# Multiplications of constants in front of TensorE's waits in a three-layer mixed kernel

## The chip, the cores and the metric

The kernel runs on one core of one Trainium2 chip. The metric is the device time of one execution in microseconds (us), from the start of the program to its end.
## What is computed

256 tokens of width 1024 go through two layers of a first block and one layer of a second. Cut to what matters:

```python
# first block: conditioning by adaLN, two layers
mod = silu(c) @ ada_w[layer] + ada_b[layer]        # six rows of 1024: shifts, scales, gates
h = modulate(rmsnorm(x, g), sh1, sc1)
# layer 0: Mamba-2 scan (both directions) beside 2-D neighbourhood attention, 16 heads
# layer 1: mLSTM, 8 heads, both directions
x = x + g1 * rmsnorm(mixer(h))                     # then the same around the MLP of width 4096
# second block, one layer
proj = rmsnorm(x) @ w_in                           # Fox attention, S5, HGRN2 and three gates
merged = g0 * (y_fox @ wb0) + g1 * (y_s5 @ wb1) + g2 * (y_hg @ wb2)
x = x + merged @ w_out
x = x + cross_attention(rmsnorm(x), rmsnorm(mem))  # 4 heads of width 256
x = x + swiglu(rmsnorm(x), w_gate_up, w_down)
```

All is float32. The large products are made from two halves of each operand (high and low), in three passes.

## The kernel before, in words

All weights come as one stream of chunks (4 tiles of 128 rows by 512 columns, 1 MB), loaded by SP into a ring of seven. For each chunk ScalarE writes the high half (`split_hi`, L1193), VectorE the low half (`split_lo`, L1204), and TensorE multiplies: L1020 where the tokens are stationary ("tok"), L1028 where the weights are ("feat"). `Product` is one weight matrix; `PRODUCTS` gives their order: mem, in0, out0, up0, down0, in1, out1, up1, down1, in2, glu, fox_out, s5_out, hg_out, mix_out, xq, xo, gate_up, swi_down. Results go to PSUM banks in pairs, and ScalarE and VectorE take them.

Smaller work (scans, softmax heads, norms) is woven between the chunks: each engine runs a generator per stage, and `Woven` advances those of the guests by a table of due steps (`paced`). So the order on every engine is fixed when the program is built, and an engine that waits holds up all that stands behind it. At the end of each stage of `all_stages` the engines meet (`meet`, L4226: drain, then wait for all three).

The names that the change touches:

- `guest_columns` (L979 to L990): the adaLN rows. VectorE sums a weight chunk over its rows (L1115, L1118) in eight steps; TensorE then adds over the partitions with a matrix of ones (L987, two columns each). There are 24 such guests, n = 0 to 23, spread over mem, in0, up0, down0, in1, out1 and up1.
- `PostProduct` and `Join`: the end of a mixer or an MLP and the norm that starts the next part. After a meeting VectorE makes the rate (L495 to L509), adds to x (L1453), ScalarE squares (L1430), TensorE transposes x in four banks (L1410), VectorE makes the second rate, TensorE lays it out as a row (L1416), and VectorE and ScalarE make the operand (L1471, L1441, L1464), tile by tile. `GainRow` (L1313) lays out the gate's row. There are four joins: before up0, in1, up1 and in2.
- `TurnHalves` and `LateNorm`: transposes of the merged branches and of x (L810) for mix_out, xq and gate_up.
- `Ssd`: the products of C and B (L1845) and the transposes of the convolved x (L1859). ScalarE makes `silu_in` (L1924) and `x_taken` (L1934).
- `Neighbours`: per head scores (L2159), softmax on VectorE and ScalarE, transposes of the shares (L2169), values (L2185). `Mlstm.turn` (L2438), `Hgrn` (L3094), `QkNorm` for Fox (L3259, after GpSimd's L3243) and `CrossAttention` (sums L3785, scores L3794, transposes L3805) are of the same kind.

The order of waits in four of these places, by the program: in `Ssd` half 1, `silu_in` at 3, then `x_taken`; in `TurnHalves`, `ready(j)` (the product's group), then `freed` (`key_in` at 4, from L3707 and L3709); in the sums of `CrossAttention`, ScalarE's and VectorE's take of the queries, then `probs_taken`; in the Fox transposes, `qk_scaled`, then `copied`.

Of the kernel before, what the change touches and what calls it, by code (L numbers as in the profile page):

```python
# [65 lines left out]
def ada_groups(layer, part0, part1):  # L66
# [32 lines left out]
          "out1": [3], "up1": [3, 9]}  # L99
FIRST_PARTS = [(0, 0), (1, 0), (0, 1), (1, 1)]  # L100
# [437 lines left out]

class MemLead(Stage):
# [257 lines left out]
class TurnHalves(TurnIn):  # L797

    def __init__(self, k, src, scale, ready, freed=()):  # L800
        super().__init__(k, src, KD, k.h_hi, k.h_lo, scale, ready)
        self.freed = freed
# [49 lines left out]
class LateNorm(TurnHalves):  # L852

    def __init__(self, k, gain, halves, junk, small, rate_row=None):
# [3 lines left out]
        super().__init__(k, k.x, lambda f: gain[:, f:f + 1], lambda j: halves(j // 2))  # L859
# [60 lines left out]
class Product(Stage):  # L920
# [9 lines left out]
    def __init__(self, k, name, src, act_out, dve_out, act_after=None, dve_after=None, is_split=False,  # L930
                 guest=None, lead=()):
        super().__init__(k)
        self.name, self.lead = name, lead
# [58 lines left out]
    def tensor(self, pe):  # L992
# [46 lines left out]
        if self.own:  # L1039
            self.guest_columns(pe, len(self.own) - 1)  # L1040

# [296 lines left out]
class PostProduct(Product):  # L1338

    def __init__(self, k, name, src, y, junk, small, guest=None):
        super().__init__(k, name, src, True, True, guest=guest)
        self.y, self.junk, self.small = y, junk, small
# [41 lines left out]
class Join(Stage):  # L1385
# [14 lines left out]
    def tensor(self, pe):  # L1400
        k, m = self.k, self.m
        if self.gain is not None:
            self.gain.lay_out(pe)
        for j in range(4):
# [7 lines left out]
        for wait in self.post.taken():  # L1412
            pe.wait_ge(*wait)
        pe.wait_ge(*m["rate_in"].at(2))
# [3 lines left out]
        mm.then_inc(m["rate_laid_out"].sem, 1)  # L1418

# [392 lines left out]
class Ssd(Stage):  # L1812
# [18 lines left out]
    def tensor(self, pe):  # L1831
# [8 lines left out]
        for _ in range(6):  # L1840
            yield
        pe.wait_ge(*m["silu_in"].at(1))
# [8 lines left out]
        for half in range(2):  # L1851
            pe.wait_ge(*m["silu_in"].at(half + 2))
            for t in range(TT):
                if half == 0:
                    pe.wait_ge(*m["cb_taken"].at(t + 1))
                else:
                    pe.wait_ge(*m["x_taken"].at(t + 1))
# [273 lines left out]
class Neighbours(Stage):  # L2131
# [20 lines left out]
    def tensor(self, pe):  # L2152
# [199 lines left out]
class Mlstm(Stage):  # L2352
# [31 lines left out]
    def tensor(self, pe):  # L2384
# [45 lines left out]
        def turn(h, products):  # L2430
            pe.wait_ge(*m["head_gated"].at(4 * (h // 2) + 4))
            pe.wait_ge(*m["ml_copied"].at(products))
            if h >= 1:
                pe.wait_ge(*m["mixed_lo"].at(2 * h))
            for f in range(2):
# [119 lines left out]
def layer1_stages(k, mods, base, small, guest, post, more):  # L2555
# [62 lines left out]
    def act_after(act, st, i):  # L2618
        kind, n = order[i]
        if kind == "o":  # L2620
# [10 lines left out]
                  lead=(join, Columns(k)))  # L2631
    gate.follow(in1)
    cell = Mlstm(k, qT, kT, v, o, sel, gate, h, e, sc, sm, junk, hi, lo, first, k.guests, o_in)
    out1 = PostProduct(k, "out1", cell, y, junk2, small, guest)
# [417 lines left out]
class Hgrn(Stage):  # L3052
# [30 lines left out]
    def tensor(self, pe):  # L3083
# [4 lines left out]
        for i, c, half in self.steps():  # L3088
            if i >= 2:
                pe.wait_ge(*m["took"].at(i - 1))  # L3090
            pe.wait_ge(*m["ops"].at(i + 1))
# [125 lines left out]
class QkNorm(Stage):  # L3217
# [514 lines left out]
class CrossAttention(Stage):  # L3732
# [38 lines left out]
    def tensor(self, pe):  # L3771
        k, m = self.k, self.m

        def sums(g):
# [4 lines left out]
            else:  # L3779
                pe.wait_ge(*m["probs_taken"].at(2))  # L3780
# [143 lines left out]
def block2_stages(k, base, small, keep, s5, post):  # L3924
# [93 lines left out]
    def glu_act_after(act, st, i):  # L4018
# [14 lines left out]
                        [key_norm.m["key_in"].at(4)])  # L4033
# [3 lines left out]
    norm_x = LateNorm(k, k.par("norm_x"), halves(mix_out), rows(at_gl + TT * D), small[:, 80:96])  # L4037
# [38 lines left out]
def all_stages(k, bias, kept):  # L4076
# [78 lines left out]
    out0 = PostProduct(k, "out0", src, y, junk, small)  # L4155
# [33 lines left out]
def mlp(k, layer, mod, base, small, guest, post, more=()):  # L4189
# [17 lines left out]
    down = PostProduct(k, f"down{layer}", Operand(None, uo.hi, uo.lo, hidden.made), y, junk, small, guest)  # L4207
# [98 lines left out]
```

## Time and profile before

| | us |
|---|---|
| median of three runs | 1708.2 (1707.31 to 1708.4) |
| the profiled execution | 1710.6 |
| its span, first to last instruction | 1708.8 |
| TensorE busy | 1574.6 (92%) |
| VectorE busy | 1162.8 (68%) |
| ScalarE busy | 791.3 (46%) |
| GpSimd busy | 59.2 (3%) |

The busy share in 40 slices of 42.7 us each, in tenths, with the granted clock of TensorE and the share of the DMA engines:

```profile
PE   6978997998999979999899997999989989899998
...
DVE  6788866447776596676777566899873585556653
...
PEclk9978998998999989999999998999998999999999
DMA  9775552323766645434546553322332343244552
```

A row of the chain of work names an engine, a tile and a line with its share of the span. A row of the waits reads: who waited, for what, how long in total, how often, the longest. A row of a table by stretches gives the stretch in us from the span's start, its length, the busy time and number of instructions of each engine, the granted clock, the share of the DMA engines and what they moved. A row of the timeline gives start, duration, engine, line, operation, output and inputs, with the idle time before it and its cause in brackets.

### The profile page before, as it was taken

How to read it: one execution, taken by the hardware profiler on the slowest of the kernel's cores; microseconds unless marked ns; L12 is line 12 of the kernel's file. 1: busy time of each engine (PE TensorE's matmuls, PEld its weight loads, DVE VectorE, ACT ScalarE, POOL GpSimd, SP SyncE). 2: the span in 40 equal slices, each digit the busy share in tenths (PEclk: the TensorE clock that was granted, in tenths of full speed). 3: DMA queues.
4: the chain of work that ended last, by engine and by line, in shares of the span. 5: the costliest groups of instructions: out<-in, count | busy, mean ns of one | idle time of the engine just before them, and what ended most of it. 6: DMA issues, size and time to landing. Idle time of an engine off the chain costs nothing.

```text
span 1708.8 us, 22579 instructions
## 1 busy us (share of the span) xinstructions
PE 1574.6 (92%) x9002; PEld 1330.9 (78%) x9002; DVE 1162.8 (68%) x1837; ACT 791.3 (46%) x1069; POOL 59.2 (3%) x72
## 2 busy tenths in 40 slices
PE   6978997998999979999899997999989989899998
PEld 5768885568998778987699886866765678789997
DVE  6788866447776596676777566899873585556653
ACT  4453464445453344545355533655533544344442
POOL 0000000000000000000000003440010000000000
PEclk9978998998999989999999998999998999999999
DMA  9775552323766645434546553322332343244552
GB/s 389 304 272 201 222 199 94 114 99 105 277 234 246 268 176 221 148 124 138 206 167 229 177 193 123 125 98 99 123 124 74 148 148 136 86 145 177 182 187 74
DMA packets 41367, 292.83 MB, mean 171 GB/s; under 512 B 4528, under 2 KB 4784, under 8 KB 6704
## 3 DMA queue, kind: packets, MB, share of 16 engines
q1 hardware_dynamic: 40112, 284.04, 45.1%
q10 hardware_dynamic: 1152, 7.34, 1.1%
q8 instruction: 73, 1.20, 0.3%
q14 instruction: 30, 0.25, 0.0%
HBM read 288.22 MB, written 3.15 MB: 171 GB/s over the span
## 4 chain that ended last, share of the span: by engine, by line
PE 72%; DVE 17%; ACT 5%; issue 3%; DMA 2%; POOL 1%; DVEq 0%; SPq 0%; ACTq 0%; POOLq 0%
PE ps L1020 31%; PE ps L1028 26%; DVE ring_at_lo L1204 5%; ACT w_hi L1193 2%; DVE arena_at L1118 2%; PE ps L2886 1%; DMA ring_at<-stream 1%; PE ps L2427 1%; DVE arena_at L2008 1%; PE ps L3094 1%; PE ps L1883 1%; PE ps L2185 1%; PE ps L987 1%; PE ps L2873 1%; PE ps L2159 1%
## 5 line engine op out<-in xcount | busy, mean ns | idle before, releaser
L1204 DVE TENSOR_TENSOR ring_at_lo<-ring_at,w_hi 128x2048 fp32r<-128x2048 f32 (+1 forms) x218 | 495.8, 2275 | 212.9 <-ACT w_hi L1193 212.8
L1193 ACT ACTIVATE w_hi<-ring_at 128x2048 fp32r<-128x2048 f32 (+1 forms) x218 | 414.5, 1902 | 244.0 <-PE ps L1020 158.1
L1028 PE MATMUL ps<-h_hi,w_hi 128*128 128x256 f32 x1440 | 419.2, 291 | 8.7 <-DVE hT_at_lo L1464 6.4
L1028 PE MATMUL ps<-h_hi,ring_at_lo 128*128 128x256 f32 x1440 | 419.6, 291 | 0.0
L1028 PE MATMUL ps<-hT_at_lo,w_hi 128*128 128x256 f32 x1440 | 414.8, 288 | 0.0
L1020 PE MATMUL ps<-w_hi,arena_at_lo 128*128 128x512 f32 x1232 | 395.9, 403 | 3.7 <-ACTq L4226 2.5
L1028 PEld LDWEIGHTS ps<-h_hi,w_hi 128*128 128x128 f32 x1440 | 283.0, 197 | 18.9 <-issue 18.5
L1020 PEld LDWEIGHTS ps<-w_hi,arena_at_lo 128*128 128x128 f32 x1232 | 233.7, 193 | 61.5 <-issue 6.2
L1028 PEld LDWEIGHTS ps<-h_hi,ring_at_lo 128*128 128x128 f32 x1440 | 281.2, 195 | 0.0
L1028 PEld LDWEIGHTS ps<-hT_at_lo,w_hi 128*128 128x128 f32 x1440 | 279.0, 194 | 0.3
L1020 PE MATMUL ps<-ring_at_lo,arena_at_lo 128*128 128x512 f32 x616 | 246.5, 400 | 0.0
L1020 PE MATMUL ps<-w_hi,h_hi 128*128 128x512 f32 x368 | 155.9, 424 | 0.0
L1020 PE MATMUL ps<-ring_at_lo,h_hi 128*128 128x512 f32 x368 | 146.2, 397 | 0.0
L1020 PE MATMUL ps<-w_hi,hT_at_lo 128*128 128x512 f32 x368 | 146.1, 397 | 0.0
L1020 PEld LDWEIGHTS ps<-ring_at_lo,arena_at_lo 128*128 128x128 f32 x616 | 117.7, 191 | 27.2
L1118 DVE SCALAR_TENSOR_TENSOR arena_at<-ring_at,cond,arena_at 128x512 f32<-128x512 f32 x168 | 125.9, 749 | 3.9
L1020 PEld LDWEIGHTS ps<-w_hi,h_hi 128*128 128x128 f32 x368 | 70.5, 192 | 24.0 <-issue 10.6
L1020 PEld LDWEIGHTS ps<-ring_at_lo,h_hi 128*128 128x128 f32 x368 | 70.1, 190 | 17.5
L1020 PEld LDWEIGHTS ps<-w_hi,hT_at_lo 128*128 128x128 f32 x368 | 70.4, 191 | 13.2
L2934 POOL TENSOR_SCALAR arena_at<-con,arena_at 128x256 f32<-128x256 f32 x16 | 12.1, 753 | 1087.6 <-DVEq L4226 1049.3
L987 PE MATMUL ps<-ones,arena_at 128*128 128x2 f32 x192 | 25.2, 253 | 22.9 <-DVE arena_at L1118 22.9
L987 PEld LDWEIGHTS ps<-ones,arena_at 128*128 128x128 f32 x192 | 25.4, 203 | 26.0 <-DVE arena_at L1118 25.5
(458 smaller groups left out, 1664.0 us busy)
## 6 DMA issues: line engine op xcount, KB each, us to landing
ring_at<-stream SPq DMA_DIRECT2D x266, 1024.0 KB, 4.8
arena_at<-bias ACTq DMA_DIRECT2D x4, 768.0 KB, 6.1
kept<-arena_at ACTq DMA_DIRECT2D x2, 1024.0 KB, 11.9
arena_at<-kept ACTq DMA_DIRECT2D x2, 1024.0 KB, 7.5
arena_at<-mem SPq DMA_DIRECT2D x1, 1024.0 KB, 7.5
x_res<-x SPq DMA_DIRECT2D x1, 1024.0 KB, 17.4
out<-x_res SPq DMA_DIRECT2D x2, 512.0 KB, 2.8
con<-consts SPq DMA_DIRECT2D x1, 640.0 KB, 22.7
```

The source lines that it names most:

```text
L987: mm = pe.matmul(k.ps[:, ADA, 2 * q:2 * q + 2], k.guest_acc[:, n % 2, q * P:(q + 1) * P], k.ones[:, :], start=True, stop=True)
L1020: mm = pe.matmul(k.ps[:, bank + t, :], x, w, start=first and n == 0, stop=last and n == 2)
L1028: mm = pe.matmul(k.ps[:, bank + q // 2, (q % 2) * TOK:(q % 2 + 1) * TOK], w[:, q * P:(q + 1) * P], x, start=first and n == 0 and q % 2 == ...
L1118: ins = dve.scalar_tensor_tensor(acc, w, cond, acc, ALU.mult, ALU.add)
L1193: act.activation(k.w_hi[:, s % HI, 0:n, :], k.ring[:, c % RING, 0:n, :], ACT.Identity).then_inc(k.hi_done, 1)
L1204: dve.tensor_tensor(k.w_lo[:, c % RING, 0:n, :], k.ring[:, c % RING, 0:n, :], k.w_hi[:, s % HI, 0:n, :].bitcast(F32), ALU.subtract).then_i ...
L1883: mm = pe.matmul(k.ps[rows, 6, 0:TOK], self.xt[:, s, h * HP:(h + 1) * HP], self.e[:, h % 3, s * TOK:(s + 1) * TOK], start=s == 0, stop=s == 1)
L2008: st(dve.scalar_tensor_tensor(self.xc[:, j, :], src, w, self.xc[:, j, :], ALU.mult, ALU.add))
L2159: mm = pe.matmul(k.ps[:, 4 + h % 2, t * TOK:(t + 1) * TOK], self.q(h, t), self.keys(h), start=True, stop=True)
L2185: mm = pe.matmul(k.ps[rows, ADA, 0:TOK], self.v(h, s), self.pt[:, h % 2, s, :], start=s == 0, stop=s == 1)
L2427: mm = pe.matmul(k.ps[:, 6 + t, 0:MDV + 2], a, b, start=j == 0, stop=j == len(parts) - 1)
L2873: mm = pe.matmul(k.ps[:, 4 + i % 2, c * TOK:(c + 1) * TOK], self.bT[rows, c, q * P:(q + 1) * P], self.uT[rows, q, :], start=True, stop=True)
```

## The change

A helper `keep_busy(pe, k, bank, n)` issues n multiplications of the identity by 256 columns of ones into a PSUM bank; nothing reads the results. It is called in front of waits of TensorE, with a count for each place; where two waits stand together, the one that frees the bank now comes first. There are 174 such multiplications in all. At the ends of out0, down0, in1, out1 and down1 they stand ahead of the meeting, behind two waits that are new there.

```diff
+GUEST_FILL = {0: 8, 1: 4, 2: 3, 4: 15, 6: 4, 18: 3, 19: 3}
...
+def keep_busy(pe, k, bank, n):
+
+    for _ in range(n):
+        pe.matmul(k.ps[:, bank, 0:TOK], k.con("ident"), k.con("ones"), start=True, stop=True)
...
# MemLead.tensor
         pe.wait_ge(self.k.ident_in, 16)
+        keep_busy(pe, self.k, self.turn.bank, 7)
         pe.wait_ge(self.k.mem_in, 16)
...
# TurnHalves.turn_pair; merged has fill [(0, 3), (2, 3)], norm_x [(2, 5)]
-        for wait in [*self.ready(j), *self.freed]:
+        for wait in self.freed:
+            pe.wait_ge(*wait)
+        keep_busy(pe, self.k, 4 + j, self.fill.get(j, 0))
+        for wait in self.ready(j):
             pe.wait_ge(*wait)
...
# Product.guest_columns
-            pe.wait_ge(*k.guest_step(n, KD))
             if n >= 1:
                 pe.wait_ge(k.guest_took, n)
+            keep_busy(pe, k, ADA, GUEST_FILL.get(n, 0))
+            pe.wait_ge(*k.guest_step(n, KD))
...
# Product.tensor, at its end; end_fill is 4 for out0 and in1, 2 for down0, out1 and down1
+        if self.end_fill:
+            n = self.first_group + len(self.kinds) - 1
+            pe.wait_ge(k.act_took, k.act_groups[n])
+            pe.wait_ge(k.dve_took, k.dve_groups[n])
+            keep_busy(pe, k, self.pair(len(self.kinds) - 2), self.end_fill)
...
# Join.tensor, before the transposes, before rate_in, and after the row is laid out
+        keep_busy(pe, k, 4, 2 if self.gain is not None else 8 if self.shift is not None else 12)
...
+        keep_busy(pe, k, self.bank, 1 if self.shift is not None and self.gain is None else 2 if self.gain is not None else 3)
         pe.wait_ge(*m["rate_in"].at(2))
...
+        keep_busy(pe, k, self.bank + 1, 3)
...
# Ssd.tensor
+        keep_busy(pe, k, 4, 6)
         pe.wait_ge(*m["silu_in"].at(1))
...
         for half in range(2):
+            if half == 1:
+                pe.wait_ge(*m["x_taken"].at(1))
+                keep_busy(pe, k, 4, 6)
             pe.wait_ge(*m["silu_in"].at(half + 2))
...
# Neighbours, turn(h)
-            pe.wait_ge(*m["shares_in"].at(h + 1))
             if h >= 1:
                 pe.wait_ge(*m["probs_taken"].at(h))
+            keep_busy(pe, k, 6, {0: 17, 7: 2, 9: 2, 11: 2}.get(h, 0))
+            pe.wait_ge(*m["shares_in"].at(h + 1))
...
# Mlstm, turn(h): the same with bank 5 and 4 for h == 6, ahead of head_gated
# Hgrn: keep_busy(pe, k, 4, 4) at i == 4, ahead of ops
# QkNorm.tensor
+        pe.wait_ge(*self.hgrn.m["copied"].at(2))
+        keep_busy(pe, k, 4, 11)
         pe.wait_ge(*m["qk_scaled"].at(TT))
-        pe.wait_ge(*self.hgrn.m["copied"].at(2))
...
# CrossAttention, sums(g), g == 1
+                pe.wait_ge(*m["probs_in"].at(1))
+                keep_busy(pe, k, 4, 3)
                 pe.wait_ge(*m["probs_taken"].at(2))
```

## Rows read from the trace of the kernel before

**Rows 1.** Span with mean clock; the page's chain of work, by engine.

```profile
core 0: 1708.8 us, clock 0.958
...
PE 72%; DVE 17%; ACT 5%; issue 3%; DMA 2%; POOL 1%; DVEq 0%; SPq 0%; ACTq 0%; POOLq 0%
```

**Rows 2.** TensorE's waits: total us, times, longest.

```profile
PE ps L987 <- DVE arena_at L1118: 22.9, 8, 8.7
...
PE ps L2169 <- DVE arena_at L2236: 13.3, 4, 8.8
...
PE ps L3259 <- POOL arena_at L3243: 5.9, 1, 5.9
...
PE ps L1859 <- ACT arena_at L1934: 4.8, 1, 4.8
...
PE ps L810 <- DVE x_res L3480: 4.7, 2, 3.0
...
PE ps L810 <- DVE arena_at L3707: 2.0, 1, 2.0
```

**Rows 3.** Table by stretches, TensorE alone: 15 stretches at half clock, and their sum.

```profile
65.30:68.70 3.40, 3.40 (x9) 0.50 0.87 352
...
607.10:611.40 4.30, 4.30 (x20) 0.50 0.02 4
...
1063.80:1068.80 5.00, 4.96 (x23) 0.50 0.00 0
...
1478.40:1485.20 6.80, 6.80 (x20) 0.50 0.00 0
sum 57.20, PE 57.10; mean PE 3.81
```

**Rows 4.** Timeline of TensorE around 1287 us: the clock rises between the pairs.

```profile
1286.17 0.63 PE L1020 MATMUL ps<-w_hi,hT_at_lo 128*128 128x512 f32 x1
1286.59 0.63 PE L1020 MATMUL ps<-ring_at_lo,h_hi 128*128 128x512 f32 x1
...
1288.46 0.39 PE L1020 MATMUL ps<-ring_at_lo,h_hi 128*128 128x512 f32 x1
1288.69 0.40 PE L1020 MATMUL ps<-w_hi,h_hi 128*128 128x512 f32 x1
```

**Rows 5.** Tables by stretches, all engines: PE, PEld, DVE, ACT, POOL, clock, DMA.

```profile
20.00:40.00 20.00, 15.87 (x61) 12.75 (x60) 14.64 (x24) 10.46 (x13) 0.00 (x0) 0.83 1.02 416
...
100.00:150.00 50.00, 40.79 (x268) 39.50 (x269) 49.66 (x91) 17.82 (x17) 0.00 (x0) 0.80 0.55 204
610.00:650.00 40.00, 35.79 (x253) 34.05 (x253) 38.93 (x55) 19.21 (x20) 0.00 (x0) 0.94 0.62 237
```

**Rows 6.** Instructions of line L2064: min/median/max ns, first and last start.

```profile
L2064 PE MATMUL ps<-arena_at,con x16: 379/379/454, 260.0 to 263.3; 128*128 128x256 f32 x16
```

**Rows 7.** Timeline of ScalarE from 156 us.

```profile
156.09 1.06 ACT L1924 ACTIVATE arena_at<-arena_at 128x1024 f32<-128x1024 f32 x1 [11.90 <-DVE arena_at L2010]
157.06 1.89 ACT L1193 ACTIVATE w_hi<-ring_at 128x2048 fp32r<-128x2048 f32 x1
158.86 1.06 ACT L1934 ACTIVATE arena_at<-ps 128x512 f32<-128x512 f32 x2
```

**Rows 8.** Timeline around 1398 and around 1477 us.

```profile
1397.61 1.65 DVE L3707 TENSOR_SCALAR arena_at<-ps,par 128x256 f32<-128x256 f32 x4
...
1476.26 0.69 DVE L3769 TENSOR_TENSOR arena_at<-arena_at 128x512 f32<-128x512 f32 x1
...
1477.05 2.32 PE L3785 MATMUL ps<-ones,arena_at 128*128 128x2 f32 x16 [2.06 <-issue]
```

**Rows 9.** Table by stretches, TensorE alone, in and around two joins.

```profile
594.40:597.70 3.30, 1.80 (x16) 1.00 0.62 218
...
853.80:857.10 3.30, 3.30 (x16) 0.50 0.00 0
857.20:860.50 3.30, 0.84 (x6) 1.00 0.00 0
```

More of the change, by code:

```diff
@@ L797, with __init__ @@
 class TurnHalves(TurnIn):
[L800 removed]
+    def __init__(self, k, src, scale, ready, freed=(), fill=()):
         super().__init__(k, src, KD, k.h_hi, k.h_lo, scale, ready)
[L802 removed]
+        self.freed, self.fill = freed, dict(fill)
     def turn_pair(self, pe, j):
[L805 removed]
+        for wait in self.freed:
+            pe.wait_ge(*wait)
+        keep_busy(pe, self.k, 4 + j, self.fill.get(j, 0))
+        for wait in self.ready(j):
             pe.wait_ge(*wait)
@@ L852, with __init__ @@
 class LateNorm(TurnHalves):
-    def __init__(self, k, gain, halves, junk, small, rate_row=None):
+    def __init__(self, k, gain, halves, junk, small, rate_row=None, fill=()):
         self.m = {"half_squares": k.mark("half_squares", 2)}
@@ L858, in __init__ @@
             self.m.update({n: k.mark(n, 1) for n in ("rate_in", "rate_laid_out", "rate_row_in")})
-        super().__init__(k, k.x, lambda f: gain[:, f:f + 1], lambda j: halves(j // 2))
+        super().__init__(k, k.x, lambda f: gain[:, f:f + 1], lambda j: halves(j // 2), fill=fill)
         self.halves, self.junk, self.small, self.rate_row = halves, junk, small, rate_row
@@ L1338, with __init__ @@
 class PostProduct(Product):
-    def __init__(self, k, name, src, y, junk, small, guest=None):
+    def __init__(self, k, name, src, y, junk, small, guest=None, fill=0):
         super().__init__(k, name, src, True, True, guest=guest)
+        self.end_fill = fill
         self.y, self.junk, self.small = y, junk, small
@@ L1855, in tensor @@
                     pe.wait_ge(*m["cb_taken"].at(t + 1))
-                else:
-                    pe.wait_ge(*m["x_taken"].at(t + 1))
+                elif t == 1:
+                    pe.wait_ge(*m["x_taken"].at(2))
                 for q in range(4):
@@ L2434, in turn @@
                 pe.wait_ge(*m["mixed_lo"].at(2 * h))
+            keep_busy(pe, k, 5, 4 if h == 6 else 0)
+            pe.wait_ge(*m["head_gated"].at(4 * (h // 2) + 4))
             for f in range(2):
@@ L2631, in layer1_stages @@
                   lead=(join, Columns(k)))
+    in1.end_fill = 4
     gate.follow(in1)
     cell = Mlstm(k, qT, kT, v, o, sel, gate, h, e, sc, sm, junk, hi, lo, first, k.guests, o_in)
-    out1 = PostProduct(k, "out1", cell, y, junk2, small, guest)
+    out1 = PostProduct(k, "out1", cell, y, junk2, small, guest, 2)
     out1.at_row = at_o
@@ L3090, in tensor @@
                 pe.wait_ge(*m["took"].at(i - 1))
+            if i == 4:
+                keep_busy(pe, k, 4, 4)
             pe.wait_ge(*m["ops"].at(i + 1))
@@ L4032, in block2_stages @@
                         lambda j: [(k.dve_took, k.dve_groups[hg_out.first_group + j // 2 + 1])],
-                        [key_norm.m["key_in"].at(4)])
+                        [key_norm.m["key_in"].at(4)], [(0, 3), (2, 3)])
     mix_out = DveProduct(k, "mix_out", Operand(None, k.h_hi, k.h_lo, merged.made), add_to_x(k))
     halves = lambda product: lambda half: [(k.dve_took, k.dve_groups[product.first_group + half + 1])]
-    norm_x = LateNorm(k, k.par("norm_x"), halves(mix_out), rows(at_gl + TT * D), small[:, 80:96])
+    norm_x = LateNorm(k, k.par("norm_x"), halves(mix_out), rows(at_gl + TT * D), small[:, 80:96], fill=[(2, 5)])
     at_o = at_su
@@ L4154, in all_stages @@
     src = Joined(Operand(None, norm.zs_r, norm.xc_r, norm.made), KD, Operand(None, na_hi, na_lo, na.made))
-    out0 = PostProduct(k, "out0", src, y, junk, small)
+    out0 = PostProduct(k, "out0", src, y, junk, small, fill=4)
     out0.at_row = at_c
@@ L4206, in mlp @@
     hidden.follow(up)
-    down = PostProduct(k, f"down{layer}", Operand(None, uo.hi, uo.lo, hidden.made), y, junk, small, guest)
+    down = PostProduct(k, f"down{layer}", Operand(None, uo.hi, uo.lo, hidden.made), y, junk, small, guest, 2)
     down.at_row = base + 2 * 32 * TOK
```

3 lines of the change are left out of this document (1 added, 2 removed).

## The prediction, made before the change was run

> **What bounds the kernel now.** I read the span and the clock first, then the chain of work that ended last, then TensorE's waits, then the granted clock stretch by stretch. The profiled execution has a span of 1708.8 us at a mean clock of 0.958 [rows 1]. The chain runs on TensorE for 72% of the span and on VectorE for 17% [rows 1]: a microsecond taken from TensorE counts in most places. The reader is to see two kinds of loss. One is waiting: the adaLN column sums L987 wait 22.9 us, softmax transposes L2169 13.3 us with one wait of 8.8, and so on [rows 2]. The other comes after a wait: the clock falls to 0.50, which is 1.2 instead of 2.4 GHz, and dense work then runs at half speed. Where the clock is low, multiplications of 512 columns start 0.42 us apart, a little later 0.23 [rows 4]. The change shortens no wait; it can only save the second loss.
>
> **What could be saved.** I took the 15 stretches at 0.50 in which TensorE works and is on the chain. They start at 65.3 us and end with the one at 1478.4, and hold 57.1 us of busy TensorE [rows 3]. At full clock half of it goes: 28.5 us. Five are taken down:
> - 607.1 to 611.4 (half is 2.15): from 610 to 650 VectorE is busy 38.9 of 40 us [rows 5], so what TensorE gains turns into waiting. I keep 0.8, about VectorE's idle time there.
> - 812.8 to 816.2 (1.7): chain pieces of VectorE follow; I keep 1.0.
> - 1063.8 to 1068.8 (2.5): VectorE is nearly full from 1090 on; I keep 2.0.
> - 1222.9 to 1225.8 (1.45): two more waits for VectorE follow; I keep 1.0.
> - 1478.4 to 1485.2 (3.4): its first microsecond is two-column products, which aren't bound by columns; I keep 3.0.
> These take off 3.4, so the ceiling is 25 us. Not counted at all: 100 to 150 us, where VectorE is busy 49.7 of 50 [rows 5] and the products behind the guests' waits can't move the end, and 625 to 628, for the same reason [rows 5]. Nor the start, where transfers keep the DMA engines full (1.02 from 20 to 40 us) [rows 5]. Fills in these places (guests 0, 1, 4, 6, 18, 19, the first of `Ssd`, and the seven ahead of the memory rows, which at half clock may end about when these land, at 9.8 us) neither gain nor cost. If their cover were gone, each would cost its 0.44 us.
>
> **The added work.** `keep_busy` multiplies the identity by the 256 columns of ones in plain f32. The nearest row is L2064: eight such multiplications leave 16 records that start between 260.0 and 263.3 us [rows 6], 3.3 us over 15 steps, so 0.44 us each at full clock and 0.88 at half. There are 174: 77 us more TensorE work. Each handful stands in front of a wait and runs while TensorE would idle. I set each against its wait. Head 0's 17 take 7.5 us in a wait of 8.8; the 11 ahead of the Fox transposes 4.8 in 5.9; guest 4's 15 take 6.6 in 8.7; the five of `norm_x` 2.2 in 3.0 [rows 2]. The others leave 0.2 to 2 us too, or overrun by less than 0.5 us under a transfer (guest 1, at 48 us). The end fills at the meetings (4, 2, 4, 2, 2) end before ScalarE and VectorE arrive; the waits that are new there, for the group before the last, are for products evacuated a chunk earlier. What queues behind them is TensorE's drain and its arrival at the meeting. Inside the joins the one to twelve products end before the wait on `x_joined` or `rate_in` does, and the last three run in the 2.1 us in which VectorE and ScalarE make the first operand. Waits that only change places (guest columns, the turns of `Neighbours` and `Mlstm`, the Fox transposes) stand in front of the same instruction as before and pass no transfer. Cost of all these: nothing, as long as the clock is up when they start; it is, since each follows dense work.
>
> **Three handfuls are not covered**, and here the order of the waits matters.
> - `Ssd`, second half, 6 products. The code now waits for `x_taken` at 1 first, then fills, then waits for `silu_in` at 3. ScalarE makes silu_in (L1924) at 156.1, then splits weights, and only then makes x_taken (L1934, from 158.9) [rows 7]. The wait that ends last is in front of the fill. Transposes L1859 and the dense products behind them start later by 6 x 0.44 = 2.6 us, with any clock: at half clock the fill is twice as long, but then the real work behind it has the higher clock.
> - `TurnHalves` for the merged branches, pair 0, 3 products. They come after `freed` (key_in at 4, made by L3707), which is what ended the 2.0 us wait [rows 2, 8]; the group that they should precede was there already. 1.3 us.
> - `CrossAttention`, second sums, 3 products. In front of them stands the wait for VectorE's take of the queries (L3769, until 1476.95); L3785 starts at 1477.05 [rows 8]. The waits that come after the fill are long met. 1.3 us.
> Sum of the exposed: 5.2 us, on the chain at all three (TensorE's dense work follows). Bounds: 0 if the next engine would have been late by that much, 5.2 as worked out, 10.4 if they also keep half clock alive; the rows stand for the middle.
>
> **How much of the ceiling is reached.** A wait of 1.55 us at 594.4, followed by L1313's products with the same identity, left the clock at 1.00 [rows 9]; so work on constants counts. The waits after filling have 0.3 to 1.5 us left, but there are several in a row in the joins, and head 0's stretch keeps 1.3 us empty. The three waits of 1.5 us at heads 7, 9 and 11 (four waits less the long one [rows 2]) were followed by 0.50 at two, at 321 and 348 us, and not at the third: which one loses it can't be read off beforehand. I take 0.7 of the ceiling, between 1/3 (only the waits filled almost whole) and 1: 25 x 0.7 = 17.5 us.
> Here a page speaks against it. First the row: 16 transposes from 853.8 to 857.1 fill that stretch at 0.50, and right after it the clock is 1.00 [rows 9]; transposes do wake it. The Trainium skill, "TensorE: Matmul & The Clock Gate", section on PE-mode transpose, says that a transpose "doesn't count as PE-busy the same way". The trace disagrees. If the rule held in the joins, they would stay at half clock for all fills.
>
> **Sum.** 1708.8 - 17.5 + 5.2 = 1696.5 us of span. The profiled execution took 1710.6, 1.8 more than its span, and the median of the three runs is 1708.2; off that median 12.3 us gives 1696 us.
>
> **Rivals.**
> 1. All hold: 25 - 5.2 = 19.8, so 1688 us. For it: fills are sized to their waits. Against it: 1096 and 1304, where nothing is filled, and the short rests in the joins.
> 2. The gain is swallowed by the next wait for VectorE or ScalarE. For it: VectorE is full in stretches [rows 5], and the softmax heads end on VectorE. Against: TensorE has 72% of the chain. A third more of the gain lost: 1708.2 - 11.5 + 5.2 = 1702 us.
> 3. Joins don't hold, since they are mostly transposes between short fills: that takes 406.6, 607.1, 860.8 and 1063.8 out, (1.7 + 0.8 + 1.6 + 2.0) x 0.7 = 4.3 us, so 1700 us. The page's rule named above would bring this about.
> 4. Only a third of the ceiling, because what is left of each wait is still enough to drop the clock: 8.3 against 5.2, so 1705, and with half of that again lost to VectorE 1708 us: no difference. I take 1707.
> 5. Slower: products of a constant are not seen as work. Then the clock falls inside the long handfuls. Head 0: some 7 of 17 at 0.44, ten at 0.88, 11.9 us against 8.8, 3 late; Fox and the joins 1 to 2 together; the exposed three 5.2. Nothing is saved: 1708.2 + 10 = 1718 us. It decides if the clock is at 0.50 before head 0's transposes, at 280 us. L1313 speaks against it [rows 9].
>
> **Chances.** Forecast 0.50 (own range 1690 to 1703), rival 1 0.13, rival 2 0.11, rival 3 0.05, rival 4 0.12, rival 5 0.09. The range of 8 in 10 goes from 1686 to 1709; it leaves out rival 5 and the tails. A measurement of this kernel can tell about 0.2%, 3.4 us, from no change. Faster by more than that: the first four but a small tail, 0.77; within: 0.14; slower: 0.09.
>
> **What would show it.** The mean clock near 0.98 instead of 0.958. Clock 1.00 right after 280, 406, 860, 1282, 1410, 1437 us (shifted by the gains). The wait before L1859 the same with 2.6 us of fills between it and the transposes; 1.3 us of fills directly in front of L810 pair 0 and of L3785. Wrong if the clock still falls after filled waits, if waits for VectorE grow by what was won, or if the fills take other than 0.44 us.

## The result: time and profile after

| | kernel before | changed kernel |
|---|---|---|
| median of 5 runs | 1708.4 us (1707.31 to 1712.97) | 1698.71 us (1696.43 to 1702.12) |
| ratio, 95% interval | | 0.9943 [0.9928, 0.9959] |
| profiled execution, its span | 1710.6, 1708.8 us | 1697.6, 1695.8 us |

The change makes the kernel 0.57% faster. The forecast was 1696 us (range 1686 to 1709), with 0.77 on faster; the span was forecast as 1696.5 and came out at 1695.8. The number was nearly met, but by errors that cancel, as the sections below show.

Span and clock, and the page's chain by engine, which answer to [rows 1]. The mean clock rose from 0.958 to 0.988; the chain is nearly the same (PE 72% before).

```profile
core 0: 1695.8 us, clock 0.988
...
PE 71%; DVE 17%; ACT 5%; issue 3%; DMA 2%; POOL 1%; DVEq 0%; SPq 0%; ACTq 0%; POOLq 0%
```

TensorE's waits of after (total us, times, longest), answering to [rows 2]. L999 is the guests' L987 of before, L2195 the softmax transposes L2169, L3290 the Fox transposes L3259; L543 is the new multiplication in `keep_busy`. A wait that was filled is short now: 22.9 us became 13.9, 13.3 became 2.6, 5.9 became 1.2. The other engines arrive no earlier: these waits are now filled with products. Three are written against L543 itself, which means that the handful stands behind the wait and not inside it.

```profile
PE ps L999 <- DVE arena_at L1135: 13.9, 8, 3.0
...
PE ps L543 <- ACT arena_at L1959: 3.2, 1, 3.2
...
PE ps L2195 <- DVE arena_at L2262: 2.6, 4, 1.3
...
PE ps L543 <- issue: 2.1, 1, 2.1
PE ps L543 <- DVE arena_at L3738: 1.9, 1, 1.9
PE ps L3124 <- DVE arena_at L3210: 1.9, 1, 1.9
...
PE ps L3290 <- POOL arena_at L3273: 1.2, 1, 1.2
```

Table by stretches of after, TensorE alone (stretch, its length and PE busy, with the number of records that lie in it wholly or in part, clock, DMA share, GB/s). It answers to [rows 3], in order of time: places that were at half clock, and among them the new ones, at 0.50.

```profile
66.30:69.70 3.40, 3.40 (x19) 1.00 1.01 426
160.80:164.20 3.40, 3.40 (x9) 0.50 1.01 414
282.40:286.50 4.10, 2.98 (x15) 1.00 0.00 0
320.60:324.00 3.40, 2.97 (x14) 1.00 0.66 222
347.90:351.30 3.40, 2.96 (x14) 1.00 0.68 280
404.90:408.30 3.40, 3.40 (x31) 1.00 0.00 0
603.40:607.70 4.30, 4.30 (x36) 1.00 0.00 0
635.30:642.10 6.80, 6.67 (x32) 0.50 0.50 173
...
858.50:861.90 3.40, 3.21 (x27) 1.00 0.00 0
1059.10:1064.00 4.90, 4.21 (x34) 1.00 0.02 3
...
1253.10:1256.50 3.40, 3.40 (x12) 0.50 0.02 5
1278.00:1281.40 3.40, 3.40 (x21) 1.00 0.02 5
1346.40:1352.10 5.70, 5.69 (x27) 0.50 1.00 415
...
1428.00:1431.40 3.40, 3.40 (x31) 1.00 0.02 5
1466.40:1473.20 6.80, 6.80 (x40) 1.00 0.01 2
```

The reader is to see two things. At every place in the table that was at 0.50 and has a handful inside its wait, the clock is 1.00; outside the table guest 6's is an exception, whose four products leave 2.3 us of the wait, and behind it the clock is at 0.50 from 143.7 us for 6.8 us (for 3.4 before). And there are stretches at 0.50 where the kernel before had none: 635, 1253 and 1346 us, and 51.6 us in the front.

**Where the time went.** I took the start of the same VectorE instruction in both traces (both have 1837) and subtracted. Worked out from the traces, negative is earlier than in the kernel before; the first column is the time in the kernel before, the others are after, the same kernel once more (e0), and the experiments.

```
   before   after      e0      e1      e2      e3      e4      e5      e6      e7      e8      e9     e10
    40.31    0.93    1.00    1.22    1.26   -0.12    1.20    1.30    1.18    1.32    1.30    1.09    1.12
   103.19    1.06    2.93    1.20    1.22   -0.07    1.59    2.85    3.02    2.78    1.39   -0.16    0.48
   161.19    1.06    2.92    1.19    1.22   -0.09    1.60    2.85    3.01    2.79    1.40   -0.15    0.49
   170.01    3.18    4.74    5.08    1.71    2.69    5.05    4.70    2.20    2.07   -0.76    2.73    2.60
   262.80    3.17    4.75    5.08    1.71    2.69    5.05    4.70    2.20    2.07   -0.76    2.73    2.60
   630.07   -3.67   -2.11    6.56   -5.13   -4.16   -1.74    0.21   -4.61   -4.73   -7.56   -4.07   -4.20
   653.44   -0.77   -0.61    9.52   -2.18   -1.19   -0.32    3.16   -3.11   -3.25   -6.06   -1.13   -1.21
  1250.48   -8.44   -6.99    7.61   -8.60   -8.81   -7.91    1.06  -10.69  -10.86  -13.67   -7.48   -8.85
  1276.17   -6.89   -5.46    7.58   -7.02   -7.26   -6.33    1.06   -9.11  -10.92  -13.76   -5.89   -7.25
  1356.08  -10.51   -9.10    7.68  -10.67  -10.88   -9.70   -2.57  -12.75  -12.99  -15.77   -9.54  -10.91
  1366.16   -8.01   -9.11    7.69   -9.18   -8.22   -8.22   -0.12  -10.20  -12.99  -15.76   -8.05   -8.35
  1488.60  -12.96   -7.85   11.13  -11.06  -10.07  -13.19   -5.08  -14.59  -15.23  -22.29   -9.91  -13.28
```

For after, the column adds up to gains of 6.84 (262.8 to 630.1), 7.67 (653.4 to 1250.5), 3.62 (1276.2 to 1356.1) and 4.95 us (1366.2 to 1488.6), 23.1 in all, and to losses of 1.06 (start), 2.12 (161 to 170), 2.90 (630 to 653), 1.55 (1250 to 1276) and 2.50 us (1356 to 1366), 10.1 in all. The net is 13.0 us, the difference of the spans.

### The profile page after: what moved, and what is told of

Read it like the earlier page. It is cut to its first block, busy times and chain, and to the rows that moved or that the text cites. A ratio compares the mean times of both kernels' runs of the same rounds, so it can differ in the third digit from the quotient of the medians.

```text
span 1695.8 us, 23259 instructions
## 1 busy us (share of the span) xinstructions
PE 1615.9 (95%) x9348; PEld 1363.5 (80%) x9348; DVE 1162.2 (69%) x1837; ACT 790.4 (47%) x1069; POOL 59.2 (3%) x72
## 4 chain that ended last, share of the span: by engine, by line
PE 71%; DVE 17%; ACT 5%; issue 3%; DMA 2%; POOL 1%; DVEq 0%; SPq 0%; ACTq 0%; POOLq 0%
PE ps L1032 31%; PE ps L1040 26%; DVE ring_at_lo L1221 5%; ACT w_hi L1210 2%; DVE arena_at L1135 2%; DMA ring_at<-stream 2%; PE ps L2453 1%; DVE arena_at L2033 1%; PE ps L2914 1%; PE ps L1908 1%; PE ps L3124 1%; PE ps L999 1%; PE ps L2211 1%; PE ps L2184 1%; PE ps L2901 1%
## 5 line engine op out<-in xcount | busy, mean ns | idle before, releaser
L1040 PE MATMUL ps<-h_hi,w_hi 128*128 128x256 f32 x1440 | 413.9, 287 | 4.5 <-DVE hT_at_lo L1485 2.5
L1040 PE MATMUL ps<-h_hi,ring_at_lo 128*128 128x256 f32 x1440 | 415.0, 288 | 0.0
L1040 PE MATMUL ps<-hT_at_lo,w_hi 128*128 128x256 f32 x1440 | 409.9, 285 | 0.0
L1032 PE MATMUL ps<-w_hi,arena_at_lo 128*128 128x512 f32 x1232 | 389.3, 397 | 3.2 <-DVEq L4259 0.8
L1040 PEld LDWEIGHTS ps<-h_hi,w_hi 128*128 128x128 f32 x1440 | 277.7, 193 | 15.3 <-issue 14.8
L1032 PEld LDWEIGHTS ps<-w_hi,arena_at_lo 128*128 128x128 f32 x1232 | 228.5, 188 | 59.6 <-issue 7.7
L1040 PEld LDWEIGHTS ps<-h_hi,ring_at_lo 128*128 128x128 f32 x1440 | 275.9, 192 | 0.0
L1040 PEld LDWEIGHTS ps<-hT_at_lo,w_hi 128*128 128x128 f32 x1440 | 273.7, 190 | 0.3
L543 PE MATMUL ps<-con 128*128 128x256 f32 x346 | 85.2, 393 | 12.4 <-DMA con<-consts 3.9
L543 PEld LDWEIGHTS ps<-con 128*128 128x128 f32 x346 | 66.0, 197 | 24.6 <-DMA con<-consts 3.9
```

The costliest lines, as they stand in the source:

```text
L543: pe.matmul(k.ps[:, bank, 0:TOK], k.con("ident"), k.con("ones"), start=True, stop=True)
L1032: mm = pe.matmul(k.ps[:, bank + t, :], x, w, start=first and n == 0, stop=last and n == 2)
L1040: mm = pe.matmul(k.ps[:, bank + q // 2, (q % 2) * TOK:(q % 2 + 1) * TOK], w[:, q * P:(q + 1) * P], x, start=first and n == 0 and q % 2 == ...
```

## The experiments

Each is an edit of the changed kernel, and cuts of lines are marked by three dots; e0 is that kernel unedited, once more. Three groups shared a chip each; the medians of the kernel before were 1707.74 us (e0 to e3), 1710.72 us (e4 to e7) and 1710.31 us (e8 to e10), so ratios are compared, not times.

**e0: the same kernel again.**

> The changed kernel once more, as the measure for the others on this chip. Mean clock near 0.987, time about 1698 us, 0.6% under the kernel before.

Measured: 1702.43 us, ratio 0.9956 [0.994, 0.9973]; profiled span 1701.0 us. The ratio agrees with 0.9943. The profile shows where 5 us of difference between two executions of one kernel come from. The column e0 ends at -7.85 and after at -12.96; from 1366 to 1488 us after gains 4.95 and e0 loses 1.26. In e0 the clock falls behind three waits there (from 1390.6, 1448.7 and 1469.1 us), in after behind none. So one column alone says little about fractions of a microsecond at the end; a single step of it, where several kernels agree, does.

**e1: products of two columns in the handfuls, 1.8 times as many.**

```
 def keep_busy(pe, k, bank, n):
-    for _ in range(n):
-        pe.matmul(k.ps[:, bank, 0:TOK], k.con("ident"), k.con("ones"), ...)
+    for _ in range((9 * n + 4) // 5):
+        pe.matmul(k.ps[:, bank, 0:2], k.con("ident"), k.con("ones")[:, 0:2], ...)
```

> Every product of keep_busy has 2 columns instead of 256, and there are 1.8 times as many, so each handful lasts about as long (two-column products with a full weight load took 0.24 us each in L3785 of before, against 0.44). The outputs are the same. My theory, that the gain comes from the clock which streaming columns hold: the clock falls behind the waits as in the kernel before, mean 0.955 to 0.965, and the time is that of before plus the three uncovered handfuls, about 1712 us (1707 to 1717). The rival, that an engine which merely has instructions to run keeps its clock, or that the gain comes from the changed order of the waits: mean clock 0.985 and 1698 us.

Measured: 1723.85 us, ratio 1.0097 [1.0083, 1.0111]: slower than the kernel before. Head 0's handful was to take the same time in both kernels; it takes 7.61 us in after and 9.32 us in e1, and there it runs past the end of the wait. First its line in the timeline of after (start, us, records), then in that of e1.

```profile
274.65 7.61 PE L543 MATMUL ps<-con 128*128 128x256 f32 x34
```

```profile
276.57 9.32 PE L543 MATMUL ps<-con 128*128 128x2 f32 x62
```

Table by stretches, TensorE alone, the start of the transposes behind the handful in after, and then in e1 the same and the whole of the handful.

```profile
282.40:286.50 4.10, 2.98 (x15) 1.00 0.00 0
```

```profile
281.00:291.00 10.00, 10.00 (x39) 0.50 0.04 5
273.00:286.00 13.00, 13.00 (x78) 0.81 0.10 42
```

In e1 TensorE is busy in all 13 us from 273 to 286, as the profile counts it, and the clock falls at 281 all the same, 4.5 us into the handful, and stays at 0.50 to 291. Behind the 256-column products it stays at 1.00. So the gain of the change is the clock, and it hangs on what the products are: covering the wait with instructions isn't enough. It is 12 us above the 1712 that I expected. The column e1 and further marks of the same two traces show where, against the kernel before. The stretches with the three exposed handfuls lose 3.9, 2.5 and 1.4 us (161 to 170, 1391 to 1402, 1475 to 1489), 7.8 in all, where I had 5.2. The joins lose 0.7, 1.6 and 0.5 (402 to 415, 857 to 870, 1060 to 1075), head 0 loses 1.3, the stretch from 630 to 653 us 3.0 and the start 1.2. Some places still gain, as that of 348.6 us (1.6), so not every handful of narrow products lost the clock. The likely reason is that these handfuls cost time and hold the clock in few places only; no run tells the parts of the 12 us apart.

**e2: without the second handful of `Ssd`** (the six products between `x_taken` and `silu_in`).

```
             if half == 1:
                 pe.wait_ge(*m["x_taken"].at(1))
-                keep_busy(pe, k, 4, 6)
```

> Without the six products behind x_taken in the second half of Ssd (the waits stay as changed). My theory, that they stand on the chain uncovered: 2.6 us faster than the changed kernel, about 1696 us, and L1859's second transposes start as soon as x_taken ends. In the profile they took 4.5 us at half clock, so by busy time alone one could expect 4.5 us; by my theory the work behind them then meets the half clock instead. The rival, that they hold or wake the clock for the dense work to 260 us: same time or slower than the changed kernel.

Measured: 1698.03 us, ratio 0.9935 [0.9921, 0.9949]. Against e0 the ratio is 0.0021 lower, with intervals that overlap. The place itself is clear. ScalarE of after around it (start, us), which answers to [rows 7], and TensorE of after:

```profile
157.15 1.06 ACT L1949 ACTIVATE arena_at<-arena_at 128x1024 f32<-128x1024 f32 x1 [13.67 <-DVE arena_at L2035]
158.12 1.89 ACT L1210 ACTIVATE w_hi<-ring_at 128x2048 fp32r<-128x2048 f32 x1
159.92 1.06 ACT L1959 ACTIVATE arena_at<-ps 128x512 f32<-128x512 f32 x2
```

```profile
160.55 4.54 PE L543 MATMUL ps<-con 128*128 128x256 f32 x12 [3.20 <-ACT arena_at L1959]
164.93 1.04 PE L1884 MATMUL ps<-con,arena_at 128*128 128x128 f32 x8
```

L1949 makes what the wait behind the handful wants, and had done so by 158.2; L1959 (`x_taken`) came last. The handful starts when the transposes could have. From the mark at 161 to that at 170 us the seven kernels that have it here in this position and in this form (after, e0, e3, e4, e5, e9, e10) lose 2.12, 1.82, 2.78, 3.45, 1.85, 2.88 and 2.11 us; e2 loses 0.49. The median of the seven, 2.12, against 0.49 is 1.6 us for six products. But e6 has these six out too, and there the same stretch is 0.81 us shorter than before: 2.9 us by that trace. So the six cost 1.6 to 2.9 us, and the 2.6 that was forecast lies between.

**e3: without the handfuls of the front** (guests 0, 1, 2, 4 and 6, the seven before the memory rows, the first six of `Ssd`).

```
-GUEST_FILL = {0: 8, 1: 4, 2: 3, 4: 15, 6: 4, 18: 3, 19: 3}
+GUEST_FILL = {18: 3, 19: 3}
...
-        keep_busy(pe, self.k, self.turn.bank, 7)
...
-        keep_busy(pe, k, 4, 6)
         pe.wait_ge(*m["silu_in"].at(1))
```

> Without the fills of the first 160 us that I take as neutral: the seven ahead of the memory rows, those of guests 0, 1, 2, 4 and 6, and the first six of Ssd. The theory that transfers and VectorE set the pace there: low clock again in stretches of the first 160 us, and a time within 1.5 us of the changed kernel (guest 2 alone could be worth 1.7). The rival, that the clock counts there too (some 20 us of busy TensorE at half clock): 5 us slower or more. A third possibility: the profile of the changed kernel reached 103 us about 1 us later than before; if an earlier start of the products makes the transfers collide, this kernel is 1 us faster.

Measured: 1699.89 us, ratio 0.9951 [0.9936, 0.9966], the same as e0. Its mark at 40 us is at -0.12, where after, e0, e1 and e2 were 0.93 to 1.26 late. I took this for the price of the front's handfuls and set out to find which; e4, e9, e10 and e8 show that it was a wrong reading.

**e4: without the seven before the memory rows.**

```
         pe.wait_ge(self.k.ident_in, 16)
-        keep_busy(pe, self.k, self.turn.bank, 7)
         pe.wait_ge(self.k.mem_in, 16)
```

> The changed kernel without the seven products ahead of the memory rows alone. In the profiles so far every kernel with all the early fills reaches the 103 us mark of before 1.1 to 2.9 us late, and the kernel without any of them 0.1 us early. Theory: the seven raise the clock before the first transposes and products, the ring's first chunks are released sooner, and the chunk that the chain waits for at 37 us then shares the full DMA engines with others and lands later. Then this kernel's mark at 40 us is back to within 0.2 us of before. Rival: guest 0's eight, or mere variation of transfers: the mark stays 1 us late. In the time this is 1 us, less than the runs scatter.

Measured: 1698.55 us, ratio 0.9927 [0.9915, 0.994]; the mark at 40 us is still 1.20 late. The seven are not the cause.

**e5: without the products inside the joins** (before the first wait on `x_joined`, before `rate_in`, and the last three).

```
-        keep_busy(pe, k, 4, 2 if self.gain is not None else 8 if self.shift is not None else 12)
...
-        keep_busy(pe, k, self.bank, 1 if ... else 2 if ... else 3)
         pe.wait_ge(*m["rate_in"].at(2))
...
-        keep_busy(pe, k, self.bank + 1, 3)
```

> The changed kernel without the products inside the four joins (before the transposes, before the second rate, after the row); the end fills stay. My theory: the clock falls again around the joins, at 406, 607, 860 and 1064 us of before, and 4 to 8 us are lost against the changed kernel: about 1704 us. The rival from the page on transposes, that joins stay at half clock with or without them: no difference, 1699 us. Their other possible effect, that they run into the waits: then this kernel is faster by some tenths of a microsecond per join, seen in the time from the meeting to the first operand.

Measured: 1705.37 us, ratio 0.9963 [0.995, 0.9977], against 0.9927 of e4 beside it, which has these products: 0.36%, 6 us. The products at the end of the stages before (the end fills) are still there. Table by stretches of e5, TensorE alone:

```profile
404.90:408.30 3.40, 2.35 (x11) 0.50 0.00 0
605.60:612.40 6.80, 5.12 (x24) 0.50 0.01 2
...
865.00:868.40 3.40, 3.40 (x18) 0.50 0.00 0
1059.30:1062.70 3.40, 2.97 (x14) 0.50 0.00 0
```

The same joins are at 1.00 in after (404.9, 603.4, 858.5 and 1059.1 in the table above). So the short handfuls between the transposes do hold the clock, and the clock in the joins needs them.

**e6: without the three handfuls that I had counted as uncovered** (e2's edit, the pair 0 of the merged branches, the second sums of the cross attention).

```
-                        [key_norm.m["key_in"].at(4)], [(0, 3), (2, 3)])
+                        [key_norm.m["key_in"].at(4)], [(2, 3)])
...
-                pe.wait_ge(*m["probs_in"].at(1))
-                keep_busy(pe, k, 4, 3)
```

> The changed kernel without the three handfuls behind the wait that ends last: six in Ssd, three at the first merged pair, three at the second sums of the cross attention. My prediction's working: 2.6 + 1.3 + 1.3 = 5.2 us less, about 1694 us. The rival: some of them pay for themselves by the clock. For the three of the cross attention the profiles so far speak for that: 1459 to 1488 us of before took 2.0 us less in the changed kernel where the clock stayed up, and 2.8 us more in its second profile where it fell. Then 1696 us, with the low clock back at 1478 us.

Measured: 1695.92 us, ratio 0.9912 [0.9898, 0.9925], against 0.9927 [0.9915, 0.994] of e4 beside it: 2.6 us better by the middles, with overlapping intervals. The timeline of after shows the two short ones in place, each behind its wait as in [rows 8]:

```profile
1391.32 1.56 PE L543 MATMUL ps<-con 128*128 128x256 f32 x6 [1.91 <-DVE arena_at L3738]
1392.72 0.60 PE L821 MATMUL ps<-con,arena_at 128*128 128x128 f32 x4
...
1466.07 1.53 PE L543 MATMUL ps<-con 128*128 128x256 f32 x6 [2.06 <-issue]
1467.44 1.84 PE L3818 MATMUL ps<-ones,arena_at 128*128 128x2 f32 x16
```

Each delays the work behind it by 1.4 us (1391.32 to 1392.72, 1466.07 to 1467.44). But the clock behind them is 1.00 in after and was 0.50 in the kernel before (from 1399.9 and from 1478.4 us, the second in [rows 3]). Over all traces with 256-column handfuls or none: at the first place the clock held in seven of the eight with the handful (not in e0) and in one of four without it (in e6; before, e7 and e8 lost it). At the second sums it held in seven of eight with the three in that place (not in e0) and in neither without any (before, e6). So a handful out of place does seem to work on the clock of what follows it. What it pays back is read from marks of the same traces. From 1475 to 1489 us after gains 2.0 and e6, with the clock at 0.50 from 1466.0, 1.6: there the three pay for themselves. From 1391 to 1408 us after loses 0.15, e6 gains 1.18, and e8, which lost the clock there, gains 0.11: the first merged pair is no better with them in any of these traces.

**e7: the handfuls moved to where the wait is, and three waits filled that had lost the clock.**

```
             if half == 1:
+                pe.wait_ge(*m["offsets_taken"].at(1))
+                keep_busy(pe, k, 6, 9)
                 pe.wait_ge(*m["x_taken"].at(1))
-                keep_busy(pe, k, 4, 6)
...
+            if g == 1:
+                pe.wait_ge(*m["probs_in"].at(1))
+                keep_busy(pe, k, 4, 4)
             pe.wait_ge(k.act_took, k.act_groups[self.first + g + 1])
             pe.wait_ge(k.dve_took, k.dve_groups[self.first + g + 1])
...
-            if i == 4:
-                keep_busy(pe, k, 4, 4)
+            if i in (4, 16):
+                keep_busy(pe, k, 4, 4 if i == 4 else 3)
...
                 if i == 0:
+                    if self.name == "glu" and f == 0:
+                        keep_busy(pe, k, bank, 5)
                     self.wait_source(pe, f)
...
-GUEST_FILL = {..., 18: 3, 19: 3}
+GUEST_FILL = {..., 18: 5, 19: 7}
```

The merged pair 0 is without its handful, as in e6. Four products stand before the second sums now, ahead of the two waits for the queries' take, and bank 6 serves the nine of `Ssd`, since bank 4 is what `x_taken` frees.

> The uncovered handfuls moved ahead of the wait that ends last, and four waits filled that are not or too little: in Ssd nine products into bank 6 before x_taken is waited for; four before the takes of the queries in the cross attention; none at the first merged pair; five ahead of the gate product glu (wait of 3.2 us); three at step 16 of Hgrn (1.9 us); guests 18 and 19 with 5 and 7 for 3 and 3. My theory, full cover: 5.2 us of uncovered time gone, and 3 to 6 us of half clock at 160, 635, 1253 and 1345 us: about 1690 us, mean clock 0.99. The rival, that what is won there ends in the next wait for VectorE: 1695 us.

Measured: 1689.79 us, ratio 0.9877 [0.9858, 0.9896]: faster than both kernels, and than e6 beside it (0.9912 [0.9898, 0.9925]) by 0.35%. In the marks the loss from 1250 to 1276 (1.55 in after) is -0.06, and that from 1356 to 1366 (2.50) is 0.00. These two are where step 16 of the Hgrn and the first product of the gated branch have their new handfuls. Of the ten changed kernels without them, eight lost the clock at each of the two places and two held it (e1 and e5 at the first, e0 and e1 at the second); e7 and e8 held it at both. The loss from 630 to 653 stays, at 1.48: seven products leave only 0.59 us of guest 19's wait, but eight products of two columns and four of 64 follow before the dense work, and the clock falls at 636.5 us all the same. In `Ssd` the moved nine bring nothing over e6, which has none there (161 to 170 us: -0.72 and -0.81); in e8, where the clock stays up, it is -2.16.

**e8: e7 without the handfuls of the front** (e3's edit on e7).

> The kernel with the moved handfuls, and without the handfuls of the front (the seven before the memory's transposes, those of guests 0, 1, 2, 4 and 6, and the six ahead of the first of the Ssd's waits). What the moved kernel was late at 103 us (+2.8 against the kernel before) goes, as it went where only the front was taken out (-0.1 there); from there on the moved kernel gained 18 us and this one should too, except that the wait at 161 us may find the clock low. Theory: what the front costs is kept to the end, mark at 103 us at 0 to +0.5, time 1687, between 1684 and 1690. Rival: the front's lateness is only a shift that the weight stream takes back anyway, so the time stays within 1 us of the moved kernel beside it (1690, 1688 to 1693), though the mark at 103 us is better by 2.8.

Measured: 1688.23 us, ratio 0.9876 [0.9856, 0.9897]; e7 had 0.9877. So the front's handfuls bring nothing and cost nothing that can be measured; the rival of this run is right about the time. Its profiled span is the shortest, 1686.5 us; that of e7, 1693.6, belongs to the longest of e7's five runs (1695.35 us), so the columns e7 and e8 don't tell the two apart. Table by stretches of e8, TensorE alone, at the two waits filled since e7:

```profile
1343.00:1352.00 9.00, 9.00 (x58) 1.00 0.77 307
1246.00:1252.00 6.00, 5.50 (x41) 1.00 0.27 113
```

The moved handful of `Ssd` in the timeline of e8: it ends 0.81 us before `x_taken` comes, and the transposes follow that at once, at full clock.

```profile
156.03 4.05 PE L543 MATMUL ps<-con 128*128 128x256 f32 x18
160.88 1.14 PE L1885 MATMUL ps<-con,arena_at 128*128 128x128 f32 x8 [0.81 <-ACT arena_at L1960]
```

The mark at 40 us is at +1.30 here, in a kernel that has no handful ahead of it, and that issues there what e3 and the kernel before issue.

**e9 and e10: without guest 0's eight, and without those of guests 1 and 2.**

```
-GUEST_FILL = {0: 8, 1: 4, 2: 3, 4: 15, ...}
+GUEST_FILL = {1: 4, 2: 3, 4: 15, ...}          (e9)
+GUEST_FILL = {0: 8, 4: 15, ...}                (e10)
```

> Only the eight products ahead of guest 0's columns are taken out. Theory: these eight delay the weight products that follow at 25 to 40 us, so the mark at 40 us goes back from +1.0 (+0.93 to +1.32 in every kernel that has them) to between -0.2 and +0.2. Rival: the lateness comes from guest 1 or later handfuls, and the mark stays at +0.9 to +1.3. For the time both expect 1697 to 1701; it is the mark that tells them apart.

> Only the handfuls ahead of the columns of guests 1 and 2 (four and three products) are taken out; guest 0's eight stay. If guest 0's eight are what is late at 40 us, the mark stays at +0.9 to +1.3; if guest 1's four are, it goes to -0.2 to +0.2. For the mark at 103 us, which was +1.1 to +2.9 with all of them: if each handful costs its own share, +0.5 less than the kernel after beside it. Time 1697 to 1701 by both.

Measured: 1697.96 us, 0.9933 [0.9913, 0.9952], and 1698.86 us, 0.994 [0.9925, 0.9954]. The marks at 40 us are 1.09 and 1.12: neither is the cause, and with e8 no handful is. Executions of the same front differ by 1.4 us there. At 103 us the eight kernels with all guests' handfuls are 1.06 to 3.02 late, and e3, e8, e9 and e10 -0.16 to 1.39. A cost of about a microsecond for the front is possible; the times of e7 and e8 don't show it, and four traces don't settle it. A table by stretches of e3 and then of e8 shows how the executions part:

```profile
31.00:38.00 7.00, 6.32 (x19) 0.51 1.02 420
50.00:55.00 5.00, 5.00 (x28) 1.00 0.89 311
```

```profile
31.00:38.00 7.00, 6.55 (x26) 0.76 1.00 412
...
50.00:55.00 5.00, 5.00 (x17) 0.50 0.86 216
```

Same instructions, and the clock is lost at another wait.

## Why the prediction was right, and where it was not

- **What bounds the kernel and what the change can save: right.** No wait of another engine's making got shorter, the clock after it did. e1 has the same waits in the same order, covered by two-column products, and the gain is gone (1.0097), so it doesn't come from the order of the waits.
- **The ceiling of 25 us: met as a sum, in part by luck.** The gains of the marks are 23.1 us, with the two short exposed handfuls in them (1.3 by the marks, 1.4), so 25.8 without. Only 21.9 of this is at places that I had counted. The other 3.9 is at three waits that I had left out: 1096 us (1.3) and 1304 (1.55), where nothing is filled and after kept the clock, and 1400 (1.1). Of the counted places two brought nothing, with 1.7 kept for each: that of 65.3 us, whose gain the marks at 60 and 103 us don't show, and that of 795.7. Behind the latter TensorE in after waits for VectorE instead, at full clock:

```profile
799.81 0.63 PE L2465 MATMUL ps<-con,arena_at 128*128 128x128 f32 x4 [1.45 <-DVE arena_at L2570]
```

  The places that I had taken down: 812.8 had 1.0 kept, and the marks around it (812.03: -0.70, 821.91: -2.09) give 1.4; 1063.8 had 2.0 kept, and from 1060 to 1090 us (-3.50, -5.67) it is 2.2; 607.1 had 0.8 kept, and from 601.65 to 610.38 us (-3.08, -3.67) it is 0.6.
- **The share of 0.7: the step that failed first.** All 15 counted places hold the clock, and 13 bring time. The three waits that I could not tell apart at heads 7, 9 and 11 are all followed by 1.00. Their 21.9 us are 0.88 of the ceiling and 4.4 more than the 17.5 that I took; the three uncounted places add 3.9.
- **Waits without enough products counted at nothing: the step that failed second, and by as much.** I summed the places that were at 0.50 in one trace, and let the places at 1.00 stand. Neither list is fixed. Guest 19's wait, step 16 of the Hgrn and the first wait of the gated branch had kept the clock in the kernel before and lost it in after; they cost 2.9, 1.55 and 2.5 us, and the start 1.06: 8.0 us. Whether the kernel before would lose them in another execution is open: it has one trace. For the gated branch here are the wait and what follows it, in the kernel before and in after (TensorE alone):

```profile
1353.60:1356.90 3.30, 0.07 (x1) 1.00 0.62 204
1356.90:1362.60 5.70, 5.68 (x48) 1.00 1.00 424
```

```profile
1343.10:1346.40 3.30, 0.06 (x1) 0.82 0.51 211
1346.40:1352.10 5.70, 5.69 (x27) 0.50 1.00 415
```

  The same wait of 3.25 us, the same work, 48 records in 5.7 us and then 27. In after the clock falls at 1345.2 us, inside the wait. The wait was in the trace of before; I passed over it because nothing was lost there. Guest 19's I had called neutral because VectorE is full from 610 to 650 us [rows 5]. In after VectorE waits 2.6 us for the products behind the guest columns (L2640 from 642.9 us), so the cover that I named is not there once TensorE is at half speed for 6.8 us.
- **The exposed handfuls, 5.2 us: the mechanism right, the sizes partly.** All three stand behind the wait that ends last, as read from the order of the waits. The two short ones delay 1.4 us each (1.3 forecast). That of `Ssd` costs 1.6 us by e2 and 2.9 by e6, around the 2.6 forecast: its six products take 4.4 us (160.55 to 164.93), nearly all at half clock, and the work behind them then runs at the higher one (e2 has the half clock there). Taking out all three changed the ratio by 0.0015 against e4, 2.6 us with overlapping intervals, half of the forecast. A part of what is missing is seen in e6's trace: at the second sums nothing is saved, since the clock is at 0.50 from 1466.0 us.
- **Sum.** -17.5 + 5.2 was forecast. With the terms as read from after's marks it is -21.9 and -3.9, +2.1 for `Ssd`, +2.7 for the short ones, and +8.0: -13.0. The 8.3 us too little in the gain and the 8.0 missing in the loss cancel; nothing in the prediction made them do so, and that is luck. The medians over runs show a little less: the ratios 0.9943 and 0.9956 are 9.7 and 7.5 us off 1708, where I had 12.3. Range and direction held.
- **Rival 1** (all hold, 1688 us) is right for the waits that are filled; e7 and e8 come to its time (0.9877 and 0.9876) once the rest is filled and the exposed are moved. **Rival 2** (swallowed by the next wait): at 607, where it had been taken off, and at 795.7 and 65.3, where it had not; 3.4 us of the ceiling, not a third. **Rival 3** (joins don't hold) falls with the clock of 1.00 in them and with e5. The Trainium skill, "TensorE: Matmul & The Clock Gate", section on PE-mode transpose, says of a transpose that "it doesn't count as PE-busy the same way"; taken at its word, the joins, which are mostly transposes, would be at 0.50. The trace disagrees, as the row at 853.8 had already done [rows 9]. **Rival 4** (a third) falls by the table and the 21.9 us. **Rival 5** (constants are not seen as work) falls for products of 256 columns, by the clock of 1.00 before head 0's transposes. With two columns its picture comes true: 1723.85 us, where it had 1718.
- **A product's price of 0.44 us** at full clock holds (0.45): 17 in 7.61 us at head 0, 9 in 4.05 us in e8.

## What to carry to other kernels

Count a clock loss at every wait of TensorE that has dense work behind it, not only at those that lost it in the one trace at hand, and fill them all: here two unfilled waits, of 1.9 and 3.25 us, and one of which its products left 2.3 us gave back 7 of 23 us. Fill a wait with wide products, and put the handful in front of the wait that ends last; read from the timeline which one that is, and give the products a bank that this wait doesn't free. Before looking for the cause of a difference of a microsecond between two traces, compare two executions of the same instructions.

## What the hardware showed that I had not expected

- TensorE busy without a gap from 273 to 286 us, with two-column products from 276.6 us on, lost the clock at 281 (e1); with 256-column products for 7.61 us (after) it did not.
- One and the same wait of 3.25 us kept the clock (1.00 from 1356.9 us, before) and lost it (0.50 from 1346.4 us, after). Between executions of the same instructions (e3 and e8, from 50 to 55 us) it is 1.00 and 0.50. Which of several waits loses the clock is not fixed: unfilled waits that had lost it before kept it in after (1096 and 1304 us), and lost it again in others (1096 in e0, e2 and e9, 1304 in e1, e7 and e8). The 5 us between the spans of after and e0 lie for the most part at such waits; whether the scatter of all runs has this cause is not shown.
